# State-space groups: SiLU behind the last exponential, low parts later, transposes waiting bank by bank, decay rows as two fp32r passes

## The reference

```python
z, xbc, dt = split(h @ w_in)
x, b, c = split(silu(dwconv1d(xbc, conv_w, conv_b)))     # x: 32 heads of 64; b, c: 4 groups of 128
dt = softplus(dt + dt_bias)
def step(s, inp):                                        # one chunk; s is the state from the context
    cum = cumsum(dt * A)
    w_end = exp(cum[-1] - cum) * dt
    s_new = exp(cum[-1]) * s + einsum('bsgh,bsgn,bsghp->bghpn', w_end, b, x)
    seg = where(tri, cum[t] - cum[s], -inf)
    w = exp(seg) * (c @ b.T) * dt
    y = w @ x + exp(cum) * (c @ s)
y = (y_forward + y_backward + d_skip * x) * silu(z)
out = rmsnorm(y by group) @ w_out
```

## Time and profile before

| | |
|---|---|
| runs | 2908.57 us median of 3 (2908.52 to 2911.18) |
| profiled execution | 2913.43 us, span 2911.6 us |
| mean granted clock | 0.981 |
| PE busy | 2697.7 us (93%) |
| DVE busy | 1943.9 us (67%) |
| ACT busy | 1091.0 us (37%) |
| POOL busy | 240.3 us (8%) |
| the four state-space groups | 2320.0 to 2630.4 us of the span |
| start of the transposes of groups 1, 2, 3 | 2401.74, 2484.97, 2564.65 us |

### The profile page before, as it was taken

How to read it: one execution, slowest core, us unless ns; L and a number is a source line. 1 busy time by engine, 2 the same in 40 slices (tenths; PEclk the granted TensorE clock), 3 DMA queues, 4 the chain that set the end, 5 groups by cost and what they waited for, 6 DMA issues and landing times.

```text
span 2911.6 us, 48608 instructions
## 1 busy us (share of the span) xinstructions
PE 2697.7 (93%) x18294; PEld 2294.3 (79%) x18294; DVE 1943.9 (67%) x3303; ACT 1091.0 (37%) x1389; POOL 240.3 (8%) x135
## 2 busy tenths in 40 slices
PE   3999999999999989999989969999999889989998
PEld 3998988899998888899868844787644667668887
DVE  6776666777777756666755382677696676664781
ACT  2434432443542434154464551433201644432211
POOL 0000000000000000000022300344200000000000
PEclk9999999999999999999999989999999999999999
DMA  8775735677575553545412201222367221113442
GB/s 308 261 286 200 294 123 191 235 276 288 211 269 225 202 187 118 188 145 204 186 59 82 73 15 44 73 94 94 140 239 278 87 73 59 59 61 128 152 164 74
DMA packets 106384, 469.15 MB, mean 161 GB/s; under 512 B 7052, under 2 KB 57304, under 8 KB 58328
## 3 DMA queue, kind: packets, MB, share of 16 engines
q1 hardware_dynamic: 106200, 466.67, 44.2%
HBM read 465.58 MB, written 1.06 MB: 160 GB/s over the span
## 4 chain that ended last, share of the span: by engine, by line
PE 48%; DVE 24%; DVEq 9%; ACT 6%; DMA 6%; issue 5%; ACTq 1%; SPq 1%; POOLq 0%
PE accs L680 7%; PE accs L695 7%; PE accs L696 7%; PE accs L697 7%; DVE panel_r L86 5%; DVEq L2870 4%; PE accs L832 4%; DMA panel<-w 3%; DVE arena L2847 3%; DVE arena L2151 2%; PE accs L1241 2%; ACT arena L76 2%; PE accs L1242 2%; PE accs L1243 2%; DVE cond_panel L2151 2%
## 5 line engine op out<-in xcount | busy, mean ns | idle before, releaser
L695 PE MATMUL accs<-normed_r,arena_r 128*128 128x256 f32 (+2 forms) x1864 | 585.2, 314 | 17.6 <-DVEq L2196 7.3
L696 PE MATMUL accs<-arena_r 128*128 128x256 f32 x2069 | 584.7, 283 | 0.0
L697 PE MATMUL accs<-normed_r,panel_r 128*128 128x256 f32 (+2 forms) x1872 | 584.3, 312 | 0.0
L86 DVE TENSOR_TENSOR panel_r<-panel,arena_r 128x1024 fp32r<-128x1024 f32 (+1 forms) x295 | 390.1, 1322 | 165.7 <-ACTq L1515 120.4
L1514 ACT ACTIVATE arena_r<-panel 128x1024 fp32r<-128x1024 f32 (+1 forms) x292 | 330.4, 1132 | 385.7 <-DMA panel<-w 143.1
L695 PEld LDWEIGHTS accs<-normed_r,arena_r 128*128 128x128 f32 (+1 forms) x1864 | 350.4, 188 | 55.2 <-issue 12.8
L696 PEld LDWEIGHTS accs<-arena_r 128*128 128x128 f32 x2069 | 389.6, 188 | 1.1 <-issue 0.2
L697 PEld LDWEIGHTS accs<-normed_r,panel_r 128*128 128x128 f32 (+1 forms) x1872 | 350.2, 187 | 23.5 <-issue 0.4
L680 PE MATMUL accs<-normed,panel 128*128 128x256 f32 x1536 | 340.5, 381 | 5.2 <-ACT normed L76 2.4
L2847 DVE SCALAR_TENSOR_TENSOR arena<-accs,vectors,arena 128x189 f32<-128x189 f32 (+2 forms) x704 | 279.4, 428 | 94.9 <-issue 66.1
L680 PEld LDWEIGHTS accs<-normed,panel 128*128 128x128 f32 x1536 | 288.8, 190 | 51.2 <-issue 4.9
(11 more groups left out here) (424 smaller groups left out, 4666.9 us busy)
## 6 DMA issues: line engine op xcount, KB each, us to landing
panel<-w SPq DMA_DIRECT2D x250, 1024.0 KB, 4.9
panel<-w SPq DMA_DIRECT2D x48, 1408.0 KB, 7.9
cond_panel<-wc SPq DMA_DIRECT2D x57, 1024.0 KB, 6.3
normed<-wc SPq DMA_DIRECT2D x43, 1024.0 KB, 6.5
arena<-wc SPq DMA_DIRECT2D x19, 1024.0 KB, 5.4
residual<-xs SPq DMA_DIRECT2D x2, 1024.0 KB, 9.6
residual<-wc SPq DMA_DIRECT2D x1, 1024.0 KB, 13.0
residual<-crows SPq DMA_DIRECT2D x2, 512.0 KB, 8.9
```

The lines of the kernel that those rows point to most:

```text
L86: i = self.eng.tensor_tensor(*a, **k)
L695: pe.matmul(out, hi[:, k, 0:m], src_hi(k), start=clear and k == 0, stop=False, skip_group_check=True)
L696: pe.matmul(out, hi[:, k, 0:m], src_lo(k), start=False, stop=False, skip_group_check=True)
L697: mm = pe.matmul(out, lo[:, k, 0:m], src_hi(k), start=False, stop=last and k == n - 1, skip_group_check=True)
```

## The change

- **Decay rows.** DVE makes an fp32r copy of `dcum`'s latent columns (`rate_hi`, over the context columns of the same memory) and the rest (`rate_lo`, over the latent columns), and an fp32r copy of the identity. Each row product is then two fp32r matmuls that accumulate, in place of one fp32 matmul. PE waits once for the three parts, ahead of group 0's first row.
- **Transposes.** They no longer wait for `ssd_yz`. Banks 1 and 0 wait for the last differences and row exponentials, banks 2 and 3 for the take that empties each. The order is 1, 0, 2, 3.
- **ACT.** The SiLU of group g+1 stands directly behind the exponential of step 7. The second z eviction and high parts 2 and 3 of g+2 stand behind it; high parts 0 and 1 stay in step 6.
- **DVE.** Step 5 makes no low part; the one of half 9 is in step 6. The four low parts of g+2 are behind the takes: one ahead of the product with z, three behind it.

```diff
         early_sum = sb("early_sum", [P, T])
+        ident_r = ctx.enter_context(nc.sbuf_tensor("identity_r", [P, P], F32R))
...
+        rate_hi, rate_lo = region(19712, 512, of=arena_r)[0:64, 0:T], region(19712, 512, of=arena_r)[0:64, T:2 * T]
...
             def ssd_group(g):
                 xc, (bc_, cc) = S_XC[g % 2], S_BCC[g % 2]
+                pe.wait_ge(S("ssd_conv"), g + 1)
                 if g >= 1:
-                    pe.wait_ge(S("ssd_yz"), g)
-                pe.wait_ge(S("ssd_conv"), g + 1)
-                for s in (1, 2, 3, 0):
+                    pe.wait_ge(S("ssd_dmin"), 8 * g)
+                    pe.wait_ge(S("ssd_erow"), 8 * g)
+                for s in (1, 0, 2, 3):
+                    if g >= 1 and s >= 2:
+                        pe.wait_ge(S("ssd_y"), 4 * g - 3 + s - 2 + 2)
                     for c in range(4):
                         mm = pe.transpose(mix[:, s, c * P:c * P + P], xc[:, c, s * P:s * P + P], ident)
...
+                if g == 0:
+                    pe.wait_ge(S("rate_parts"), 3)
                 for m in range(8):
...
-                        mm = pe.matmul(mix[:, m % 2, hh * T:hh * T + T], ident[0:64, row:row + 1].to_broadcast([64, P]), dcum[0:64, lat],
-                                       start=True, stop=True)
+                        for part, rate in enumerate((rate_hi, rate_lo)):
+                            mm = pe.matmul(mix[:, m % 2, hh * T:hh * T + T], ident_r[0:64, row:row + 1].to_broadcast([64, P]), rate,
+                                           start=(part == 0), stop=(part == 1))
...
-                    if g < 3:
+                    if g < 3 and m < 7:
                         ssd_features(g + 1, m)
                         if m < 6:
                             ssd_high(g + 1, 4 + m)
                         elif g < 2:
                             for i in range(2):
-                                ssd_high(g + 2, 2 * (m - 6) + i)
+                                ssd_high(g + 2, i)
                 if g < 3:
                     act.wait_ge(S("ssd_cv"), g + 2)
                     act.eng.activation(S_XC[(g + 1) % 2], S_XC[(g + 1) % 2], ACT.Silu)
                     for v in S_BCC[(g + 1) % 2]:
                         act.eng.activation(v, v, ACT.Silu)
                     act.drain().then_inc(S("ssd_conv"), 1)
+                    ssd_features(g + 1, 7)
+                    if g < 2:
+                        for i in range(2, 4):
+                            ssd_high(g + 2, i)
                 act.wait_ge(S("ssd_yz"), g + 1)
...
                 dve.drain().then_inc(S("rates_dve"), 1)
+                dve.tensor_copy(rate_hi, dcum[0:64, lat]).then_inc(S("rate_parts"), 1)
+                dve.tensor_copy(ident_r[:, :], ident).then_inc(S("rate_parts"), 1)
...
                     if g < 3 and m < 6:
                         ssd_conv(g + 1, m)
-                        ssd_low(g + 1, 4 + m)
-                    elif g < 2:
-                        for i in range(2):
-                            ssd_low(g + 2, 2 * (m - 6) + i)
+                    if g < 3 and m < 7 and m != 5:
+                        ssd_low(g + 1, 4 + m - m // 6)
                     if m in (3, 5, 7):
                         ssd_take(g, (m - 3) // 2)
                 ssd_take(g, 3)
                 dve.drain()
+                if g < 2:
+                    ssd_low(g + 2, 0)
                 dve.tensor_tensor(S_Y[:, 4 * g:4 * g + 4, :], S_Y[:, 4 * g:4 * g + 4, :], S_Z[g % 2], ALU.mult)\
                    .then_inc(S("ssd_yz"), 1)
+                if g < 2:
+                    for i in range(1, 4):
+                        ssd_low(g + 2, i)
...
                     for i in range(4):
                         ssd_low(1, i)
+                    dve.wait_ge(S("dt_cols"), 1)
+                    dve.tensor_tensor(rate_lo, dcum[0:64, lat], rate_hi, ALU.subtract).then_inc(S("rate_parts"), 1)
                     for g in range(4):
                         ssd_group(g)
```

## The result

The changed kernel takes 2889.44 us (median of 4, 2885.58 to 2890.93), against 2909.88 us for the kernel before in the same four rounds: a ratio of 0.9921, 95% interval 0.9909 to 0.9933, or 20.4 us less. The forecast was 2887.6, within 2882 to 2898. The profiled execution took 2889.35 us; that of before, 2913.43 us, lies 3.6 us above this median of the kernel before, so the two profiles differ by more (24.1 us) than the medians.

What follows compares the result with a forecast made beforehand. TensorE was taken to set the pace wherever not made to wait, with 25.8 us idle in the groups. Gains of 5.9 + 14.3 + 1.2 - 0.3 = 21 us off the 2908.57 median gave 2887.6, range 2882 to 2898.

Steps and rivals of the forecast that it cites:

- Rows: Decay-row matmuls: two fp32r passes take 0.67 us per row group instead of 1.06, gaining 5.9 us in 15 dense steps.
- A: Decay rows: fp32r passes take as long as fp32 ones; gain only 12.7 us, 2895.9 profiled; chance 0.10.
- C: Decay rows: each 64-row fp32r pass needs two instructions, 0.86 us more per step, giving 2914 us; chance 0.04.
- The turning point of C: Decay rows: the slower case decides from about 1.55 us per row group upward.
- the 14 gained: What the slower decay-row case sets against its losses of 13, some 4 and some 2.5 us.
- Steps 5 to 7 and the SiLU: Group ends: later low parts and earlier SiLU bring the transposes 6.0, 5.1 and 3.3 us earlier, together 14.3 us.
- The waits that were to be left: TensorE's remaining idle: about 1.6 us at each boundary and 1.9 us at output 7.
- These waits are covered and worth nothing beyond the order.: Transposes' bank 2 and 3 waits for VectorE's takes: last take at 2479.0, ahead of the SiLU's end at 2479.9.
- I add nothing: Granted clock behind each boundary: shorter idle could save a us or two; nothing added, 2 us kept each way.
- The late copy, charged 0.1 a boundary: ScalarE's copy of transposed x behind the transposes: up to 0.6 us later relative to them, charged 0.3 us in all.
- Group 3: Last group, where outputs wait on the chain: step pairs fall from about 9.0 to 8.6 us, gaining 1.2 us.
- Rival B: Boundary does not move, held by ScalarE's later parts or a dearer table load: some 8.3 us gain, 2900.3; chance 0.08.

Runs made afterwards that it cites:

- e9: Kernel before with only VectorE's order changed as in the change (low parts later): 2908.02 us, ratio 0.9981 to the kernel before.
- e3: Changed kernel with the transposes waiting for the product with z again, not bank by bank: 2894.52 us, ratio 0.9934 to the kernel before.
- e2: Changed kernel with the decay rows as one fp32 matmul each again, without the parts: 2896.95 us, ratio 0.9950 to the kernel before.
- e5: Changed kernel with high parts 2 and 3 behind ACT's copy of transposed x, their low parts behind the weighing of x: 2889.24 us, ratio 0.9916 to before.
- e6: Changed kernel with first halves of the output projection one place earlier in group 3: 2887.87 us, ratio 0.9912 to the kernel before.
- e8: Kernel before with only ScalarE's order changed (SiLU directly behind the last exponential): 2915.06 us, ratio 1.0008 to the kernel before.
- e1: Kernel before with only the decay rows changed to two fp32r passes: 2907.58 us, ratio 0.9977 to the kernel before.
- e4: Kernel before with throw-away fp32 matmuls filling TensorE's idle ahead of the transposes: 2907.79 us, ratio 0.9981 to the kernel before.
- e10: Changed kernel with throw-away matmuls ahead of outputs 6, 7 and the transposes in groups 0 to 2: 2888.30 us, ratio 0.9917 to the kernel before.
- e11: Changed kernel with high parts 2 and 3 behind ACT's copy, plus throw-away matmuls in TensorE's waits: 2887.03 us, ratio 0.9907 to the kernel before.
- e12: Changed kernel with high parts behind the copy, group 3's first halves earlier, and throw-away matmuls: 2882.79 us, ratio 0.9899 to the kernel before.

## Why the prediction was right

The forecast of the time was right, and by its own mechanism for 19.8 of the 22.6 us in the groups. That the sum came so close is in part luck: the boundaries behind the transposes gave 3.0 us more than forecast, through the clock, and the rest gave 1.6 less, most of it in group 3.

**Rows.** Right to 0.01 us: 0.66 against 0.67 per row group, four records, 5.6 against 5.9 us in the dense steps. The 0.2 us of entering and leaving a run stayed. Rivals A and C are out: a 64-row fp32r pass with a broadcast weight costs what the 128-row one does. The turning point of C, 1.55 us per row group, does not follow from its own terms (0.86 more costs 19.5, so the 14 gained are used up at 1.06 + 0.62 = 1.68); nothing hangs on it.

**Steps 5 to 7 and the SiLU.** Right: 5.9, 5.0 and 3.2 us against 6.0, 5.1 and 3.3, and e9 shows the low parts' share alone. Of the 5.9, 5.0 and 3.2 us, the last exponential gave 1.85, 1.86 and 0.5 us, forecast 1.98, 1.98 and 0.6, and the SiLU directly behind it the rest. The waits that were to be left came a little shorter, 1.5 us against 1.6 ahead of the transposes and 1.4 against 1.9 ahead of output 7. The table load stayed at 1.28 us with the SiLU 0.02 behind it. The drain of 1.38 us that the Trainium skill gives ("ScalarE: Activation LUTs", "What ACT_TABLE_LOAD costs") shows in no row here, also not directly behind an exponential (2464.44, load at 2464.50).

**"These waits are covered and worth nothing beyond the order."** Wrong. The new waits are covered, but the old one would no longer have been: with the SiLU earlier, the product with z holds the transposes, for 1.7 us in two groups and 0.5 in the third, and then the clock falls: 6.1 us in all (e3).

**"I add nothing" for the clock.** This is the term that was mis-sized. It was put at 2 us either way; in the profile it is 2.6 us at group 3's boundary, and at the other two it is what pays for the late copy. It does not come in every execution: with the same 1.5 us of idle the transposes of group 1, group 2 or both were at the lower level in e2, e5 and e6.

**The late copy, charged 0.1 a boundary.** Wrong as a wait, which is 1.4 us in groups 1 and 2: the working let the transposes last 3.5 us, as in the rows of before, and they last 1.96. Start plus 6.17 us is still when L1275 runs, which is what was forecast (6.05 and 0.1); both errors are the same error, and cancel.

**Group 3.** The pairs came out as forecast: two steps in 8.62 us (2577.92 to 2586.54) instead of 9.0. Rows 2 to 7 gained 1.4 us. The step that failed is the one not looked at, row 0 and row 1: output 0 hangs on ACT's copy of the states, which with the exponential of row 0 ends 1.9 us behind row 0 in both kernels. So the short rows gain nothing there and the wait grew from 1.8 to 2.6 us; the clock fell to 0.64 behind it, and row 0 to row 2 lost 1.6 us, which e3, with the same wait and no fall, did not lose.

**Rival B** named the right place, L1275, and the wrong size: the wait is there but costs no more than the clock gave.

## What to carry to other kernels

Where the busiest engine waits at a stage boundary, write out each engine's queue from the last common event to the release, and move everything that is not needed for the release behind it, on all engines at once: one queue moved alone can bring nothing or lose (e8), as its items become late for the others. Read the granted clock beside every wait of the matmul engine, before and behind it. A saving in front of a wait only lengthens the wait, and a longer wait can cost the clock (e1, group 3); a shorter one can give more than its own length. Where a wait can't be shortened and the clock falls behind it, filling it with throw-away matmuls is worth a try (e4), with fewer than the wait holds at the lower clock; where the clock had not fallen, it brought nothing (e10). One profile shows one execution: the clock behind the same wait differed between kernels that were the same up to there.

## What the runs showed of the hardware

- The same 16 transposes of 128 columns take 1.91 to 1.97 us at a granted clock of 1.00 and 3.65 to 3.68 at 0.50, and between these (2.7 to 3.6) where the level changed within them, in every run.
- Each idle of 2.0 us or more ahead of the transposes was followed by the lower level for all or most of them (0.50 to 0.67; before, e1, e3, e8, e9). Behind 1.5 us it came at none of the three boundaries in the changed kernel's profile, at two in e5 and in e6, at one in e2. Behind 2.6 us ahead of output 0 of group 3 it came in five profiles and not in e3. The Trainium skill, "TensorE: Matmul & The Clock Gate", section "HAM oscillation — how this bites in real kernels", tells of waits that recur in a loop and bring the lower clock in each round. The kernel before agrees, with the lower clock at all three boundaries behind 3.9 to 5.6 us; the shorter waits of the changed kernels do not bring it each time.
- With no idle ahead of them, or 0.25 us of it (e4, e10, e11, e12), the transposes always ran at the higher level.
- fp32r passes of 256 columns over 64 rows, with one weight column broadcast to 128, run like those over 128 rows: starts 0.12 us apart, and four in 0.66 us with entering and leaving.
